# One hybrid decoder step: the projection taken by token groups, with the gates and the prompt chunks written between its weight slabs

## The chip, the cores and the metric

The kernel runs on one core of a Trainium2 chip. The metric is the time of one execution on the device in microseconds (us); the median of three runs is compared. The profile is one execution recorded instruction by instruction. TensorE is PE there (PEld its weight loads), VectorE is DVE, ScalarE is ACT, GpSimd is POOL, SyncE is SP.

## What is computed

One decoder layer for 2048 prompt tokens and 32 sample tokens (8 sequences of 4), 2080 in all, D = 1024:

```python
mq, mk, mv, mo, mi, mf, sq, sk, sv = split_in_proj(x @ w_in)      # 2816 columns and 8 gate columns
# group A: mLSTM, 4 heads of 128, in chunks, with a recurrent state C, n, m
logf = log_sigmoid(softcap(mf + b_fg)); b = cumsum(logf); m_row = max(b + m, max(logD))
h = (exp(b + m - m_row) * q @ C + (q @ k.T * exp(logD - m_row)) @ v) / max(|den|, exp(-m_row))
# group B: attention over a window of 128, 8 heads of 64, sinks and a relative bias
p = softmax_with_sink(q @ k.T / 8 + bias); o = p @ v
x = layer_norm(ALPHA * x + concat(rmsnorm(h) * g * sigmoid(mo), o) @ w_out)
x = layer_norm(ALPHA * x + (silu(x @ w_gate) * (x @ w_up)) @ w_ffn_out)
```

Outputs are x for all tokens and the states and window caches. All data is float32. The large products are made of three passes over a high and a low part of each operand: `hi*xh + hi*xl + lo*xh`, where `whi` is the weight rounded by ACT and `wlo` the rest, subtracted by POOL.

## The kernel before

Five programs follow each other, each with its own block and a barrier behind it.

`project` (lines 122 to 330) holds all 2080 tokens of x, split into `xh` and `xl`, in SBUF. The weights come once, as 22 slabs of 128 columns (512 KB each, two buffers of `raw`, `whi` and `wlo`); each slab meets the five token groups of 416 tokens (TG). So there are 5 gate products and 110 slab products, each of 24 matmuls (8 blocks of k, three passes, lines 267 to 269). DVE copies each result (L329), and SP stores whole rows of `projT` in DRAM.

`gates` turns the eight gate rows into the decay terms of all 16 prompt chunks: a chain of short operations on DVE and ACT, four transposes on PE, and the relative bias table (L557, L559). It writes `xsT` to DRAM and loads the first two chunks.

`prompt` is a loop over 16 chunks of 128 tokens. SP loads a chunk with four DMAs: `inp` (1280 KB in pieces of 512 B), `kwin`, `svT`, and `xs_b`, two rows of each head spread over all partitions (512 KB). These go one chunk pair ahead. Steps of chunk c+1 are written into chunk c to fill waits: its window scores (L723), exponentials (L822) and key transposes (L746). The state of a chunk enters the next.

`sample` does the same for the 32 sample tokens and fetches the first weights of the layer. `layer` (out projection, FFN, norms) is 338 slab products of the same kind, with the same two-buffer chain of load, ACT rounding and POOL subtraction. SP issues every load and nearly every store of the kernel, in order.

Of the kernel before, what the change touches and what calls it, by code (L numbers as in the profile page):

```python
# [43 lines left out]
HJ = 384  # L63
assert NG * TG == NT and NTT * TOK == TG
# [35 lines left out]
def gate_inputs(m):  # L100

    t = {n: m.sb(n, s) for n, s in (
        ("gi", [H * NC, C]), ("gf", [H * NC, C]), ("gi_s", [H, NS]), ("gf_s", [H, NS]),
        ("small", [H * NC, 4]), ("small_s", [H, 4]), ("m0_sb", [H, DB]))}
    t["loaded"] = m.sem("g_loaded")
    return t


def load_gates(sp, io, t):

    def get(dst, src):
        sp.dma_start(dst, src).then_inc(t["loaded"], 16)

    for i, (n, bias) in enumerate((("gi", "b_ig"), ("gf", "b_fg"))):
        get(t[n][:], bass.AP(tensor=io["gateT"].tensor, offset=i * H * NT, ap=[[NT, H], [C, NC], [1, C]]))
        get(t[n + "_s"][:], io["gateT"][i * H:i * H + H, SEQ:NT])
        get(t["small"][:, i:i + 1], bass.AP(tensor=io[bias].tensor, offset=0, ap=[[1, H], [0, NC], [1, 1]]))
        get(t["small_s"][:, i:i + 1], io[bias])
    get(t["m0_sb"][:], io["m0"])


def project(nc, io, gate_in):

    with ExitStack() as ctx:
        m = Store(nc, ctx)
        XK, XR = KD // 2, 3  # L130
        xh = m.sb("xh", [P, KD, NT], F32R)
        xl = m.sb("xl", [P, KD, NT], F32R)
        xraw = m.sb("xraw", [P, XR, XK, TG])
        graw = m.sb("graw", [P, KD, P])
        raw = m.sb("raw", [P, 2, KD, P])
        whi = m.sb("whi", [P, 2, KD, P], F32R)
        wlo = m.sb("wlo", [P, 2, KD, P], F32R)
        ghi = m.sb("ghi", [P, KD, P], F32R)
        glo = m.sb("glo", [P, KD, P], F32R)
        out = m.sb("out", [P, 2, NT])  # L140
        grow = m.sb("grow", [8, 2, TG])
        acc = [m.ps(f"acc{i}", [P, 512]) for i in range(8)]
# [24 lines left out]

        @block.sync
        def _(sp):
            def load(i, s):  # L170
                sp.dma_start(raw[:, s], io["wA"][bass.ds(i * 2 + s, 1)].rearrange("a p k n -> (a p) k n")).then_inc(raw_in[s], 16)

            def load_x(h):
                sp.dma_start(xraw[:, h % XR], io["xT"][h // 2, :, h % 2 * XK:h % 2 * XK + XK]).then_inc(x_in[h % XR], 16)

            def store(i, s, tiles=None):

                sp.wait_ge(acc_free, tiles or (i * 2 + s + 2) * NG)
                sp.wait_ge(g_in, 16)
                sp.dma_start(io["projT"][bass.ds(i * 2 + s, 1)].rearrange("a p n -> (a p) n"),  # L180
                             out[:, s]).then_inc(out_free[s], 16)

            def store_gates(g):
                sp.wait_ge(acc_free, 3 * g + 1)
                sp.dma_start(io["gateT"][:, g * TG:g * TG + TG], grow[:, g % 2]).then_inc(g_stored[g % 2], 16)

            for dst, src in ((relb, io["rel_bias"]), (onehot, io["c_onehot"]), (outside, io["c_outside"])):
                sp.dma_start(dst, src).then_inc(table_in, 16)
            load_x(0)
            sp.wait_ge(g_zero, 1)  # L190
# [12 lines left out]
            for s in range(2):
                sp.wait_ge(lo_done[s], 1)
                load(1, s)
            for g in range(NG - 2, NG):
                store_gates(g)
            for s in range(2):
                store(0, s, FIRST)
            for s in range(2):  # L210
                sp.wait_ge(g_stored[s], (NG + 1 - s) // 2 * 16)
            load_gates(sp, io, gate_in)
            with sp.Fori(2, ITER) as i:
                for s in range(2):
                    sp.wait_ge(lo_done[s], i)
                    sp.wait_ge(g_in, 16)
                    load(i, s)
                for s in range(2):
                    store(i - 1, s)
            for s in range(2):  # L220
                store(ITER - 1, s)

        @block.scalar
        def _(act):
            def round_x(h):
                act.wait_ge(x_in[h % XR], h // XR * 16 + 16)
                nc.scalar.activation(half(xh, h), xraw[:, h % XR], ACT.Copy).then_inc(x_hi, 1)

            round_x(0)
            act.wait_ge(g_in, 16)  # L230
            nc.scalar.activation(ghi[:], graw[:], ACT.Copy).then_inc(g_hi, 1)
            round_x(1)
            for s in range(2):
                act.wait_ge(raw_in[s], 16)
                nc.scalar.activation(whi[:, s], raw[:, s], ACT.Copy).then_inc(hi_done[s], 1)
            for h in range(2, 2 * NG):
                round_x(h)
            for s in range(2):
                act.wait_ge(raw_in[s], 32)
                act.wait_ge(acc_full, FIRST - 1 + s)  # L240
                nc.scalar.activation(whi[:, s], raw[:, s], ACT.Copy).then_inc(hi_done[s], 1)
            with act.Fori(2, ITER) as i:
                for s in range(2):
                    act.wait_ge(raw_in[s], i * 16 + 16)
                    act.wait_ge(acc_full, (i * 2 + s) * NG)
                    act.wait_ge(g_in, 16)
                    nc.scalar.activation(whi[:, s], raw[:, s], ACT.Copy).then_inc(hi_done[s], 1)  # L247

        @block.gpsimd
        def _(pool):  # L250
            nc.gpsimd.memset(graw[:], 0.0).then_inc(g_zero, 1)
            pool.wait_ge(g_hi, 1)
            nc.gpsimd.tensor_tensor(glo[:], graw[:], ghi[:].bitcast(F32), ALU.subtract).then_inc(g_split, 1)
            with pool.Fori(0, ITER) as i:
                for s in range(2):
                    pool.wait_ge(hi_done[s], i + 1)
                    nc.gpsimd.tensor_tensor(wlo[:, s], raw[:, s], whi[:, s].bitcast(F32),  # L257
                                            ALU.subtract).then_inc(lo_done[s], 1)

        @block.tensor  # L260
        def _(pe):
            def product(bank, hi, lo, g, halves=False):
# [1605 lines left out]
```

## Time and profile before

| | us |
|---|---|
| runs | 2704.88, 2705.39, 2707.74 |
| median | 2705.39 |
| span of the profiled execution (first to last instruction) | 2705.0 |
| PE busy of it | 2549.0 (94%) |
| PEld, DVE, ACT, POOL busy | 2466.6, 1062.1, 798.0, 1082.2 |
| DMA | 314.91 MB, mean 116 GB/s |

No time of its own is recorded for the profiled execution besides its span; the span is 0.4 us under the median, so what lies around it is small. The stages by time: projection to 535.2 us, gates to about 569, prompt to about 850, sample to about 892, layer from 901.9 to the end. Busy time of PE is an average over these stages, and each has another limit.

### The profile page before, as it was taken

The numbers are of one execution on the slowest core, as the hardware profiler recorded it, in microseconds if no ns is written. First come the engines' busy times: TensorE is split into PE (matmuls) and PEld (weight loads), VectorE is DVE, ScalarE is ACT, GpSimd is POOL, SyncE is SP. The second block draws the span as 40 slices with busy tenths as digits, with TensorE's granted clock in tenths as the row PEclk, the third lists the DMA queues.
The fourth block names the chain that finished last, engine by engine and source line by source line (L and its number), as shares of the span: only waits on it lengthen the run. The fifth ranks groups of instructions, "written<-read, shape, count | busy, mean of one in ns | idle before, by whom it ended". The sixth has DMA issues, their size and how long they took to land.

```text
span 2705.0 us, 39819 instructions
## 1 busy us (share of the span) xinstructions
PE 2549.0 (94%) x14173; PEld 2466.6 (91%) x14173; DVE 1062.1 (39%) x1723; ACT 798.0 (30%) x1270; POOL 1082.2 (40%) x462
## 2 busy tenths in 40 slices
PE   8999999958888779999999999999999999999996
PEld 8999999847776779999999999999999999999996
DVE  4111111147776243333553325644157341563403
ACT  2000000047885124422332223322224222242221
POOL 1111111012223335555455554555545555455553
PEclk9999999979998779999999999999999999999998
DMA  4212111176675314433344332443324433343332
GB/s 160 96 63 76 65 72 69 48 174 151 151 151 147 113 58 141 139 115 115 108 153 142 114 124 95 148 149 120 119 96 134 167 118 116 102 127 116 119 118 68
DMA packets 164636, 314.91 MB, mean 116 GB/s; under 512 B 16124, under 2 KB 111060, under 8 KB 161092
## 3 DMA queue, kind: packets, MB, share of 16 engines
q1 hardware_dynamic: 162224, 305.34, 36.3%
q10 hardware_dynamic: 2340, 8.52, 1.1%
q8 instruction: 57, 0.93, 0.1%
q14 instruction: 15, 0.12, 0.0%
HBM read 270.80 MB, written 44.17 MB: 116 GB/s over the span
## 4 chain that ended last, share of the span: by engine, by line
issue 39%; POOL 14%; PE 11%; DVE 1%; POOLq 1%; DMA 0%; ACT 0%; DVEq 0%
POOL l_wlo L1390 14%; PE l_acc L1512 4%; PE l_acc L1514 4%; PE l_acc L1513 4%; POOLq L1387 1%; DVE nrm L1641 0%; DVE stats L1632 0%; DMA out_y<-nrm 0%; POOLq L1389 0%; PE turned L1532 0%; DVE nrm L1739 0%; DVE nxt L1654 0%; DVE nxt L1650 0%; POOL al L1397 0%; DVE mv L1635 0%
## 5 line engine op out<-in xcount | busy, mean ns | idle before, releaser
L1390 POOL TENSOR_TENSOR l_wlo<-l_raw,l_whi 128x1024 fp32r<-128x1024 f32 (+1 forms) x338 | 906.4, 2682 | 848.9 <-ACT l_whi L1419 848.9
L1512 PE MATMUL l_acc<-ah,l_whi 128*128 128x416 f32 x2080 | 733.3, 353 | 23.6 <-DVEq L1613 9.9
L1514 PE MATMUL l_acc<-ah,l_wlo 128*128 128x416 f32 x2080 | 735.6, 354 | 0.0
L1513 PE MATMUL l_acc<-al,l_whi 128*128 128x416 f32 x2080 | 728.4, 350 | 0.0
L1419 ACT ACTIVATE l_whi<-l_raw 128x1024 fp32r<-128x1024 f32 (+1 forms) x338 | 384.9, 1139 | 1134.0 <-PE l_acc L1514 1100.8
L1512 PEld LDWEIGHTS l_acc<-ah,l_whi 128*128 128x128 f32 x2080 | 392.0, 188 | 29.0 <-POOL l_wlo L1390 10.3
L1513 PEld LDWEIGHTS l_acc<-al,l_whi 128*128 128x128 f32 x2080 | 392.4, 189 | 6.3
L1514 PEld LDWEIGHTS l_acc<-ah,l_wlo 128*128 128x128 f32 x2080 | 391.6, 188 | 2.7
L1512 PE MATMUL l_acc<-hh,l_whi 128*128 128x416 f32 x880 | 311.4, 354 | 7.5 <-POOL l_wlo L1390 2.9
L1514 PE MATMUL l_acc<-hh,l_wlo 128*128 128x416 f32 x880 | 309.9, 352 | 0.0
L267 PE MATMUL acc<-xh,whi 128*128 128x416 f32 x880 | 309.3, 351 | 0.0
L268 PE MATMUL acc<-xl,whi 128*128 128x416 f32 x880 | 308.2, 350 | 0.0
L269 PE MATMUL acc<-xh,wlo 128*128 128x416 f32 x880 | 308.1, 350 | 0.0
L1513 PE MATMUL l_acc<-hl,l_whi 128*128 128x416 f32 x880 | 307.4, 349 | 0.0
L1673 DVE TENSOR_TENSOR hbuf<-silu,l_acc 128x416 f32<-128x416 f32 x110 | 64.6, 587 | 501.2 <-PE l_acc L1514 501.2
L1678 DVE TENSOR_TENSOR hl<-hbuf,hh 128x416 f32 (+1 forms) x110 | 251.9, 2290 | 12.1
L257 POOL TENSOR_TENSOR wlo<-raw,whi 128x1024 fp32r<-128x1024 f32 x22 | 56.0, 2547 | 425.1 <-ACT whi L247 364.3
L329 DVE COPY out<-acc 128x416 f32<-128x416 f32 x100 | 59.2, 592 | 393.6 <-PE acc L269 389.5
L1512 PEld LDWEIGHTS l_acc<-hh,l_whi 128*128 128x128 f32 x880 | 165.2, 188 | 12.5 <-POOL l_wlo L1390 7.3
L1513 PEld LDWEIGHTS l_acc<-hl,l_whi 128*128 128x128 f32 x880 | 165.4, 188 | 2.3
L269 PEld LDWEIGHTS acc<-xh,wlo 128*128 128x128 f32 x880 | 165.1, 188 | 2.1
L268 PEld LDWEIGHTS acc<-xl,whi 128*128 128x128 f32 x880 | 165.3, 188 | 1.4
(295 smaller groups left out, 2413.0 us busy)
## 6 DMA issues: line engine op xcount, KB each, us to landing
l_raw<-in_wB SPq DMA_DIRECT2D x260, 512.0 KB, 3.4
l_raw<-in_w SPq DMA_DIRECT2D x80, 704.0 KB, 4.1
projT<-out SPq DMA_DIRECT2D x22, 1040.0 KB, 4.0
inp<-projT SPq DMA_DIRECT2D x16, 1280.0 KB, 6.7
raw<-in_wA SPq DMA_DIRECT2D x22, 512.0 KB, 5.4
xraw<-in_xT SPq DMA_DIRECT2D x10, 832.0 KB, 4.6
mixr<-mixT SPq DMA_DIRECT2D x5, 1664.0 KB, 8.9
nxt<-in_xT SPq DMA_DIRECT2D x5, 1664.0 KB, 7.8
```

Of the source, the lines that this page charges most:

```text
L257: nc.gpsimd.tensor_tensor(wlo[:, s], raw[:, s], whi[:, s].bitcast(F32), ALU.subtract).then_inc(lo_done[s], 1)
L267: pe.matmul(acc[bank][:, 0:TG], hi[:, k], xh[:, k, xs], start=(k == 0), stop=False)
L268: pe.matmul(acc[bank][:, 0:TG], hi[:, k], xl[:, k, xs], start=False, stop=False)
L269: last = pe.matmul(acc[bank][:, 0:TG], lo[:, k], xh[:, k, xs], start=False, stop=(k == KD - 1))
L329: nc.vector.tensor_copy(out[:, s, g * TG:(g + 1) * TG], acc[(n + NG) % 2][:, 0:TG]).then_inc(acc_free, 1)
L1390: nc.gpsimd.tensor_tensor(wlo[:, s, 0:k], raw[:, s, 0:k], whi[:, s, 0:k].bitcast(F32), ALU.subtract).then_inc(S["lo_done"], 1)
L1419: nc.scalar.activation(whi[:, s, 0:k], raw[:, s, 0:k], ACT.Copy).then_inc(S["hi_done"], 1)
L1512: pe.matmul(acc[:, bank, 0:TG], whi[:, s, c], hx[:, a], start=(a == 0), stop=False)
L1513: pe.matmul(acc[:, bank, 0:TG], whi[:, s, c], lx[:, a], start=False, stop=False)
L1514: last = pe.matmul(acc[:, bank, 0:TG], wlo[:, s, c], hx[:, a], start=False, stop=(a == total - 1))
L1673: nc.vector.tensor_tensor(hbuf[:], silu[:, s], acc[:, 2 * s + 1, 0:TG], ALU.mult).then_inc(S["evac"], 2)
L1678: nc.vector.tensor_tensor(hl[:, at], hbuf[:].unsqueeze(1), hh[:, at].bitcast(F32), ALU.subtract).then_inc(S["h_split"], 1)
```

## The change

`project`, `gates` and `prompt` become one program, `mixers`. The outer loop is the token group: 5 groups of 416 tokens, and for each the 22 weight slabs are loaded, rounded and split anew, so 110 slabs pass where 22 did. Only two groups of x are in SBUF; x is loaded and split in eight visits (`VISITS`). Of the gate weights only the eight real columns of each block are rounded and subtracted, the rest is set to zero. `raw` keeps two buffers, `whi`, `wlo` and `out` have three. A store is one slab of one group (208 KB).

Everything is written out, no loop is left. A slot n holds slab n (0 to 109) on every engine; five gate products stand before slabs 0, 3, 6, 9 and 12, for the groups 0, 4, 3, 2, 1. The gates' steps stand in slots 15 to 21. Each chunk is cut into six pieces (TURN, MIX, WIN, TURN2, VALUES, OUT), and a table says behind which slab each stands: chunks 0 to 8 take seven slots, chunks 9 to 15 five. Chunks are not interleaved with each other any more, except that OUT of one shares a slot with TURN of the next. Chunks 13, 14 and 15 have bases 110, 115 and 120: there are no slabs left there. `LOADS_AT` says in which slot SP loads a chunk; a chunk whose tokens end in group g is loaded after the last slab of g is stored.

In a slot, SP issues the slab four ahead, the store, then chunk loads; ACT rounds the slab three ahead, then does its pieces; POOL splits the slab three ahead, then its pieces; PE does the product, then its pieces. The Exp of `snk` stands before the Sqrt of `root`. PSUM tiles are fewer (`kd`, `fb`, `ce`, `w01`, two `acc`). The loads for `sample` go out in slot 90. `sample` and `layer` are as they were, at fixed SBUF addresses.

```diff
-def project(nc, io, gate_in):
...
-            with pe.Fori(1, ITER) as i:
-                for s in range(2):
-                    pe.wait_ge(lo_done[s], i + 1)
-                    for g in range(NG):
...
-                        product((n + NG) % 2, whi[:, s], wlo[:, s], g)
...
+VISITS = ((0, 0), (4, 1), (3, 1), (2, 1), (1, 1), (2, 0), (3, 1), (4, 0))
+SEVEN, FIVE = (0, 2, 3, 5, 6, 7), (0, 1, 2, 3, 4, 5)
+BASES = (24, 31, 38, 46, 53, 60, 68, 75, 82, 90, 95, 100, 105, 110, 115, 120)
+PIECES = tuple(tuple(b + o for o in (SEVEN if c < 9 else FIVE)) for c, b in enumerate(BASES))
+LOADS_AT = (21, 22, 28, 43, 44, 50, 65, 66, 72, 87, 88, 93, 98, 109, 110, 113)
+PREP_AT = tuple(b if c in (0, 3, 6, 9, 13) else b - 1 for c, b in enumerate(BASES))
...
+def mixers(nc, io, keep, outs, taken, at):
...
+            def load(n):
+                sp.dma_start(raw[:, n % 2], io["wA"][n % NPROJ]).then_inc(raw_in[n % 2], 16)
...
+            def load_chunk(c):
...
+                if c in (0, 3, 6, 9, 13):
+                    last = slab_tile((0, 3, 6, 9, 13).index(c) * NPROJ + NPROJ - 1)
+                    for k in range(last - 2, last + 1):
+                        landed(k)
+                sp.dma_start(inp[:, s], io["projT"][0:20, :, tok].rearrange("t p n -> p t n")).then_inc(loaded[s], 16)
...
+            for n in range(END):
+                if n < NSLAB:
...
+                    if n + 4 < NSLAB:
+                        sp.wait_ge(lo_done, n + 3)
+                        load(n + 4)
+                    store(n)
...
+            def round_slab(n):
+                act.wait_ge(raw_in[n % 2], n // 2 * 16 + 16)
+                if n >= 3:
+                    act.wait_ge(acc_full, slab_tile(n - 3) + 1)
+                nc.scalar.activation(whi[:, n % 3], raw[:, n % 2], ACT.Copy).then_inc(hi_done, 1)
...
+            for n in range(END):
+                if n + 3 < NSLAB:
+                    round_slab(n + 3)
...
+                for c in at_piece(n, OUT):
+                    out_turned(c)
+                for c in at_piece(n, TURN):
+                    turned(c)
...
+                for c in at_piece(n + 1, TURN):
+                    scale_queries(c)
```

SP at the first of the places where two chunk loads stand in neighbouring slots (43 and 44; the same at 21 and 22, 65 and 66, 87 and 88). `raw<-in_wA` is a weight slab, the four rows from `inp` to `xs_b` are one chunk. Before, from the end of one turn of the prompt loop:

```order
L348 DMA inp<-projT 128x20x128
L350 ISA
L350 DMA kwin<-projT 128x256
L352 ISA
L352 DMA svT<-projT 128x128
L357 DMA xs_b<-xsT 128x8x128
L652 ISA
L652 DMA mixT<-mixed 128x8x128
```

and now:

```order
L310 DMA inp<-projT 128x20x128
L312 DMA kwin<-projT 128x256
L317 DMA svT<-projT 128x128
L318 DMA xs_b<-xsT 128x8x128
L280 DMA raw<-in_wA 128x1024
L299 DMA projT<-out 128x416
L310 DMA inp<-projT 128x20x128
L312 DMA kwin<-projT 128x256
L317 DMA svT<-projT 128x128
L318 DMA xs_b<-xsT 128x8x128
L280 DMA raw<-in_wA 128x1024
L299 DMA projT<-out 128x416
```

A weight slab now stands behind a whole chunk in SP's queue, and another behind two.

ACT from the end of chunk 2 to the exponentials of chunk 3 (slots 42 to 46; the whi rows are the roundings of slabs 45 to 49). `whi<-raw` is a slab's rounding, `sq` the scaled queries that PE's TURN waits for, `pw` the window's exponentials, `mixed` the OUT copy. Before, in the loop:

```order
L858 ACTIVATE hn,ssq<-m 128x128 x4
L828 ACTIVATE ptw<-w2b 128x512
L863 ACT_TABLE_LOAD
L863 ACTIVATE root<-root 128x4
L865 ACT_TABLE_LOAD
L865 ACTIVATE snk<-snk 128x8
L866 ISA
L868 ACTIVATE mixed<-w2b 128x512
L641 ISA
L822 ACTIVATE pw,psums<-sw,nmx 128x256 x2
```

and now:

```order
L630 ACTIVATE whi<-raw 128x1024 x2
L651 ACTIVATE ptw<-w 128x512 x2
L630 ACTIVATE whi<-raw 128x1024 x2
L696 ACTIVATE mixed<-ce 128x512
L657 ACTIVATE sq_133<-inp 128x512
L630 ACTIVATE whi<-raw 128x1024
L663 ACTIVATE vaug<-ce 128x4x128
L641 ACT_TABLE_LOAD
L641 ACTIVATE pw,psums<-sw,nmx 128x256 x2
L669 ACTIVATE decay<-expo,ucol 128x128 x4
```

Each piece of a chunk on ACT now stands behind the rounding of the slab three ahead: `sq_133` behind that of slab 48, `vaug` and `pw` behind that of 49.

PE where one chunk passes into the next (chunk 12 into 13). `w<-kwin` are window scores, `fb<-vs` or `w3b<-vs` the values, `hn` and `ow` the two transposes of OUT, `inp` the transposes of keys and queries. Before:

```order
L723 MATMUL w<-kwin,sq 128x256 x4
L739 MATMUL w3b<-vs,ptw 128x64 x8
L746 MATMUL m0b<-ident,inp 128x128 x4
L798 MATMUL m3b<-ident,hn 128x128 x4
L802 MATMUL w2b<-ident,ow 128x128 x4
L754 MATMUL m<-ident,inp 128x128 x4
L757 MATMUL m<-inp 128x128 x4
```

and now, behind the last product:

```order
L470 MATMUL acc<-xh_64,wlo 128x416
L502 MATMUL fb<-vs,ptw 128x64 x8
L557 MATMUL kd<-ident,hn 128x128 x4
L563 MATMUL ce<-ident,ow 128x128 x4
L483 MATMUL w<-kwin,sq_133 128x256 x4
L516 MATMUL kd<-ident,inp 128x128 x4
L519 MATMUL fb<-ident,svT 128x128
L521 MATMUL ce<-ident,inp 128x128 x4
L525 MATMUL ce<-inp 128x128 x4
```

The next chunk's window scores and key transposes (`kd<-ident,inp`) stood ahead of OUT and now stand behind it.

## Rows read from the trace of the kernel before

**Rows 1.** Windows by stage: us, busy per engine (instructions), clock, DMA share, GB/s.

```profile
12.40:535.20 522.80, 522.68 (x2760) 517.01 (x2760) 86.14 (x124) 34.95 (x29) 55.92 (x22) 1.00 0.20 75
535.20:569.70 34.50, 7.12 (x17) 3.27 (x17) 9.67 (x42) 10.15 (x24) 3.26 (x10) 0.65 0.64 172
...
600.00:800.00 200.00, 171.87 (x1358) 144.88 (x1357) 149.51 (x518) 160.71 (x480) 54.65 (x48) 1.00 0.70 155
...
902.00:906.00 4.00, 4.00 (x12) 3.82 (x13) 0.00 (x0) 0.00 (x0) 0.00 (x0) 0.50 0.34 99
...
950.00:960.00 10.00, 5.72 (x25) 4.53 (x26) 9.10 (x17) 1.51 (x4) 1.94 (x1) 0.50 0.00 0
```

**Rows 2.** The first splits, in order of time: start, length, wait.

```profile
8.27 1.89 DVE L296 TENSOR_TENSOR xl<-xraw,xh 128x1664 fp32r<-128x1664 f32 x1 [2.32 <-ACT xh L227]
9.26 3.11 POOL L253 TENSOR_TENSOR glo<-graw,ghi 128x1024 fp32r<-128x1024 f32 x1 [7.57 <-ACT ghi L231]
```

**Rows 3.** Two operations of the gates' chain.

```profile
548.45 0.55 DVE L528 TENSOR_TENSOR b_s<-b_s,gf_s 4x8 f32<-4x8 f32 x3
...
551.23 0.18 DVE L537 TENSOR_TENSOR u_s<-gi_s,b_s 4x32 f32<-4x32 f32 x1
```

**Rows 4.** SP in order of time: a chunk load, a held issue, the last store.

```profile
557.10 9.95 SPq L350 DMA_DIRECT2D kwin<-projT  x1
...
627.11 0.38 SPq L348 DMA_DIRECT2D inp<-projT  x1
...
630.84 0.38 SPq L357 DMA_DIRECT2D xs_b<-xsT  x1
...
850.11 0.38 SPq L652 DMA_DIRECT2D mixT<-mixed  x1
```

**Rows 5.** DMA issues of gates and prompt: count, size, us to landing.

```profile
inp<-projT SPq DMA_DIRECT2D x16, 1280.0 KB, 6.7
xs_b<-xsT SPq DMA_DIRECT2D x16, 512.0 KB, 9.3
...
projT<-out SPq DMA_DIRECT2D x1, 1040.0 KB, 4.2
```

**Rows 6.** The layer around one large load: SP's issues, then ACT's wait.

```profile
1402.34 0.39 SPq L1347 DMA_DIRECT2D mixr<-mixT  x1
...
1406.02 0.34 SPq L1333 DMA_DIRECT2D l_raw<-in_wB  x1
...
1413.13 1.06 ACT L1419 ACTIVATE l_whi<-l_raw 128x1024 fp32r<-128x1024 f32 x1 [5.28 <-DMA l_raw<-in_wB]
```

**Rows 7.** Groups of projection and prompt: count, busy, mean ns, idle.

```profile
L329 DVE COPY out<-acc 128x416 f32<-128x416 f32 x100 | 59.2, 592 | 393.6 <-PE acc L269 389.5 <-DMA projT<-out 4.1
L257 POOL TENSOR_TENSOR wlo<-raw,whi 128x1024 fp32r<-128x1024 f32 x22 | 56.0, 2547 | 425.1 <-ACT whi L247 364.3 <-ACT whi L241 60.8
...
L822 ACT ACTIVATE pw<-sw,nmx 128x256 f32<-128x256 f32 x96 | 47.7, 499 | 14.4 <-DVE nmx L896 14.1
...
L863 ACT ACT_TABLE_LOAD x12 | 15.4, 1283 | 0.2
...
L695 POOL TENSOR_TENSOR expo<-xs_b,causal 128x512 f32<-128x512 f32 x12 | 15.3, 1274 | 2.6 <-DMA xs_b<-xsT 2.6
L839 ACT ACTIVATE decay<-expo,ucol 128x128 f32<-128x128 f32 x48 | 15.2, 389 | 0.0
```

**Rows 8.** PE: the last chunk's window scores, the sample's first.

```profile
827.40 1.14 PE L723 MATMUL w<-kwin,sq 64*128 64x256 f32 x8
...
852.84 0.37 PE L1120 MATMUL s_sc<-ident,s_inp 128*32 128x128 f32 x1 [3.50 <-PEq L591]
```

**Rows 9.** Neighbours in time on POOL and DVE in the first chunk.

```profile
588.92 1.04 POOL L702 TENSOR_TENSOR gate<-gate,gml 128x512 f32<-128x512 f32 x1
...
589.04 0.94 DVE L896 TENSOR_SCALAR nmx<-mx 128x2 f32<-128x2 f32 x1
...
833.32 0.17 DVE L896 TENSOR_SCALAR nmx<-mx 128x2 f32<-128x2 f32 x1
```

More of the change, by code:

```diff
@@ new lines, in mixers @@
+        own = t.sb("own", [R, C])
+        gx, gxs = t.sb("xs", [R, 2, C]), t.sb("xss", [H, 2, NS])
+        ones_r = t.sb("ones_r", [R, C])
+        m_last = t.sb("m_last", [H, DB])
+        m_end = t.sb("m_end", [1, H])
+        ends = t.sb("ends", [1, 2, H, NC])
+        after = t.sb("after", [1, H, NC])
+        before = t.sb("before", [1, H, NC])
+        inherited = t.sb("inherited", [R, 1])
+        anti = t.sb("anti", [P, P])
+        hank = t.sb("hank", [P, 8, 2 * W])
+        srow = t.sb("srow", [32, 132])
@@ L715, in _, with product @@
         @block.tensor
         def _(pe):
-            def window_scores(c, s, r):
-                wait(pe, "nmx_ready", c, r)
-                for g in range(2):
-                    gp = slice(64 * g, 64 * g + 64)
+            def product(k, hi, lo, v, split):
+                bank, x = acc[k % 2], VISITS[v][1]
+                if k >= 2:
+                    pe.wait_ge(acc_free, k - 1)
+                for a in range(KD):
+                    if split and a % XK == 0:
+                        pe.wait_ge(x_split, 2 * v + a // XK + 1)
+                    pe.matmul(bank[:, 0:TG], hi[:, a], xh[x][:, a], start=(a == 0), stop=False)
+                    pe.matmul(bank[:, 0:TG], hi[:, a], xl[x][:, a], start=False, stop=False)
+                    last = pe.matmul(bank[:, 0:TG], lo[:, a], xh[x][:, a], start=False, stop=(a == KD - 1))
+                last.then_inc(acc_full, 1)
@@ L722, in window_scores, with slab @@
+            def slab(n):
+                gr = n // NPROJ
+                pe.wait_ge(lo_done, n + 1)
+                product(slab_tile(n), whi[:, n % 3], wlo[:, n % 3], (0, 4, 5, 6, 7)[gr], n % NPROJ == 0)
+            def window_scores(c, r):
+                s = c % 2
+                for gr in range(2):
+                    gp = slice(64 * gr, 64 * gr + 64)
                     for a in range(2):
-                        last = pe.matmul(w01[:, g, a * 256:a * 256 + 256], sq8[gp, r + a], kwin[gp, s],
+                        last = pe.matmul(w01[:, gr, a * 256:a * 256 + 256], sq8[gp, r + a], kwin[gp, s],
@@ L774, in chunk @@
                 wait(pe, "kw_ready", c)
-                wait(pe, "pt_copied", c, 2)
-                for h in range(H):
-                    last = pe.matmul((m3, m0)[h // 2][:, (h % 2) * 129:(h % 2) * 129 + 129], kw[:, h], vaug[:, h],
-                                     start=True, stop=True)
-                last.then_inc(S["state_up"], 1)
-                wait(pe, "sv_ready", c)
-                window_values(c, s, 0)
-                turn_window(c, 2, w2)
-                window_values(c, s, 1)
@@ new lines, in mixed, with window, values @@
+                for h in range(H):
+                    last = pe.matmul(update[h], kw[:, h], vaug[:, h], start=True, stop=True)
+                last.then_inc(S["state_up"], 1)
+            def window(c):
+                wait(pe, "pt_copied", c, 2)
+                window_scores(c, 2)
+                wait(pe, "st_ready", c)
+                window_values(c, 0)
+                window_values(c, 1).then_inc(S["first_values"], 1)
+            def values(c):
+                window_values(c, 2)
+                window_values(c, 3).then_inc(S["swa_out"], 1)
@@ L803, in chunk @@
                 last.then_inc(S["o_turned"], 1)
-            pe.wait_ge(zeroed, 4)
-            pe.wait_ge(loaded[0], 64)
-            turn_keys(0, 0)
-            wait(pe, "sq_ready", 0)
-            window_scores(0, 0, 0)
-            with pe.Fori(0, NC // 2 - 1) as i:
-                for s in range(2):
-                    chunk(i, s, True)
-            for s in range(2):
-                chunk(NC // 2 - 1, s, s == 0)
+            pe.wait_ge(ext_table, 48)
+            pe.matmul(fb[0:8, 0:HJ], relb[:], onehot[:], start=True, stop=True).then_inc(ext_full, 1)
```

1232 lines of the change are left out of this document (602 added, 630 removed).

## The prediction, made before the changed kernel ran

> **What bounds the kernel now.** First the windows by stage [rows 1]. From 12.4 to 535.2 us PE is busy 522.68 of 522.80 us at granted clock 1.00, so the projection is PE's own work: 115 products, 4.546 us each. The DMA share is 0.20 there. The gates, to 569.7, are a chain of small operations: PE works 7.12 of 34.5 us at clock 0.65. The prompt is a loop of about 16.6 us a chunk (12 table loads, one a chunk, in 200 us [rows 7]); those 200 us have 171.87 us of PE, 144.88 of weight loads, 160.71 of ACT, and the DMA share is 0.70. So 28 us of 200 are waits of PE, and the chain of 34.5 us is nearly all wait. That is what placing this work between products can fill. Sample starts at 852.84 us [rows 8] and needs the last chunk's output; everything behind it, 1852.2 us to the end of the span of 2705.0, is untouched. So the whole question is when sample starts, against 852.8.
>
> **The start.** Before, PE's first product waited for `glo`, whose subtraction on POOL took 3.11 us from 9.26 [rows 2], to 12.4. Now only the eight real gate columns of each block are subtracted, so x's own split, ending at 8.27 + 1.89 = 10.16, is last: PE starts at about 10.3, 2.1 us earlier.
>
> **PE's work.** The 115 products stay, 522.8 us. A chunk's work costs between 12.1 us (weight loads, 144.88/12) and 14.3 (PE busy, 171.87/12). Busy includes matmuls that stand in the pipe while the next waits for its weights; in a piece that runs in one go behind a product, starts follow the weight loads. I take 12.1; the upper end would add 13 x 2.2 = 29 us. Behind slabs stand chunks 0 to 12; chunk 0 has no state and half a window (about 2.5 us less): 13 x 12.1 - 2.5 = 154.8. The gates' PE work is 7.12 us at clock 0.65, so 4.6 at full clock; I take 4.5. Sum: 10.3 + 522.8 + 154.8 + 4.5 = 692.4 us at the end of slab 109, with no wait at all. Before, chunk 12 is done only three chunks ahead of 850, near 800; so some 108 us are to be had at this point.
>
> **The other engines.** In a slot of 4.55 + 1.73 = 6.3 us ACT has a rounding (1.06 us [rows 6]) and a seventh of 13.4 us (160.71/12), POOL a split (2.547 us [rows 7]) and a seventh of 4.6, DVE a copy (0.592) and a seventh of 12.5. All stay under 60% on average. The sums don't bound; order can.
>
> **Loads.** One slab of 512 KB for each slot, besides the chunks: DMA goes from a share of 0.20 to about 0.65. That by itself fits. But a chunk load is issued from 627.11 to 630.84 [rows 4], 3.7 us, and its last part lands 9.3 us after issue [rows 5]: 13.0 us, of which about 10.5 are transfer (estimate: 16.6 us a chunk at share 0.70, less the stores). SP issues the load of slab n+4 behind it. Rows of the layer show what a load behind a large one does: `mixr` went out at 1402.34, `l_raw` at 1406.02, and ACT stood 5.28 us for `l_raw`, until 1413.13 [rows 6]: 7.1 us after issue. And with two chunk loads close together one issue, `kwin`, held SP 9.95 us [rows 4]. In the order of ACT, the scaled queries of chunk 3 stand behind the rounding of slab 48, its exponentials behind that of slab 49, and PE's TURN and MIX wait for these.
>
> **One pair of chunk loads, step by step** (slots 43 and 44, clock zero at the end of slot 43). The first load waits until the store of slab 43 has landed, about 3 us (1040 KB took 4.2 [rows 5]). It is issued to 6.7 and has landed at 16. Slab 48 stands behind it: landed 18, rounded 19, queries 19.6. PE wants them at TURN, behind product 46, at 2 x 6.3 + 4.55 = 17: it waits about 3. Chunk 4's load is next in line, 10.5 us of transfer; slab 49 lands at 29.5, is rounded at 30.6. Behind that come `vaug`, a table load (1.28 [rows 7]), eight `pw` of 0.5 and four `decay` of 0.39: 38. MIX stands behind product 48, at 29.7 + 3: it waits 5.5. So 9 us (rounded up) a pair, and there are four pairs. Slots 43/44 and 65/66: 18. Slots 21/22: the slots behind them have no pieces and last 4.55 instead of 6.3, so four slots give 7 us less cover, and the gates' chain of 34.5 us stands in seven slots of 4.55 (31.9): 3 late, in part the same wait; together 17. Slots 87/88: chunks of five slots, MIX one slot earlier, against longer slots: 13. The single loads in 93 and 98: 2 each, 4. Together 52 us. Behind long waits PE's clock falls: after sample it worked 4.00 of 4.00 us at 0.50 [rows 1], a loss of 2 us; four times that, 8. So 692.4 + 60 = 752.4. Of all terms this 60 is the least sure; 10 is its lower end (only the gates' chain and a little), 70 the upper.
>
> **The end.** Chunk 13 is loaded when the last slab is stored: copy and issue of `out` about 1.0 (the copy is 0.592 [rows 7]), landing 2.5 for 208 KB, load 13.0: 16.5 us with nothing beside them. To 768.9. Chunks 13, 14, 15 then have no product to cover their waits. Before's last chunk, from its window scores at 827.40 to the store at 850.11 [rows 8, 4], took 22.7 us without a next chunk beside it. In the new order the next chunk's window scores and key transposes stand behind OUT, so all three cost that: 68.1. PE is busy about half of it, and at 5.72 busy of 10 the clock was 0.50 [rows 1], so their 9 us of matmuls on the chain take 4.5 more each: 13.5. To 850.5. From the store to sample's first matmul 2.7: **853.2**, 0.4 later than before.
>
> So the span is 2705.4, and the median, 0.4 above the span before, 2705.8: I say **2706 us**. The gain between the slabs goes into waits of ACT's rounding, an open load and three uncovered chunks.
>
> **Rivals.**
> *A, the forecast*: slab loads stand in line behind chunk loads. For it: [rows 6] and the held issue. Its own range is 2690 to 2722 (waits of 45 to 70, tail of 20 to 25 a chunk).
> *B, the transfers share*: slabs overtake or share with the chunks, so the wait is 10 instead of 60, and sample starts at 803: **2656**. For it: the DMA queues are idle a third of the time, and a wait of 52 us was worked out from few rows, with a slack of three slots that needs only a few us more to hide all. Against it: in [rows 6] the later load landed after the earlier one.
> The Trainium skill ("DMA: Bandwidth & Descriptors", section "Queues, rings and completion order") says that each DMA engine takes descriptors in the order of its ring, though a later one may finish first, and speaks so against this change. The row of 5.28 us agrees; by strict order the waits are the 52 us, without it B.
> *C, slower*: POOL's split runs in every slot, 2.55 us long, and a small DVE operation beside a POOL operation stretches: `nmx` took 0.94 us beside `gate` of 1.04, against 0.17 else [rows 9]. Beside a split it may be held up to 2.4 us, and `nmx` gates the exponentials, those the transposes of TURN2 and VALUES. In 13 chunks once: 31 us more than A, **2737**. It decides only if `pw` is already later than PE: from about 3.8 us after the end of the slab. Against it: seven slots per chunk leave a slot between most pieces. The bound of 14.3 us a chunk for PE's work ends at the same time.
> The gates' small operations (0.55 and 0.18 us [rows 3]) are open to the same, but are counted as a chain already. That the pieces would not stand between slabs at all is excluded by the orders: the rounding and the pieces alternate.
>
> **How the numbers follow.** A 0.45, B 0.33, C 0.22. A measurement of this kernel tells about 0.2% (5.4 us) from no change. Of A, 0.12 falls below 2700, 0.15 within and 0.18 above 2711; B is all faster, C slower but for 0.02. So faster 0.45, same 0.17, slower 0.38. The range of 8 in 10 holds A, and most of B and of C: 2650 to 2738; A alone is 2690 to 2722.
>
> **What the changed profile would show.** Sample's first matmul near 853. PE's first product near 10.3. Before slab 109's end (at 752) PE waits of some 5 us at TURN and MIX of the chunks behind a pair, ended by ACT, with ACT's rounding waiting for DMA `raw`: if these are missing, B. `nmx` of 2 us and more beside `wlo`, and waits ended by it: C. Products that take more than 4.55 at clock 1.00 would break the PE term. Behind slab 109 a hole of some 16 us ended by DMA, then three chunks of 27 us at a clock of about 0.5; if they take 20, I am 20 us too slow. I am wrong in kind if the three-slab lookahead absorbs the chunk loads, or if waits stand where I have none (x's reload, `out`'s stores).

## The result: 63 us slower

The changed kernel takes 2769.7 us (median of 4 runs, 2767.8 to 2771.3) against 2706.2 before, now also the median of 4: a ratio of 1.0233, 95% interval 1.0218 to 1.0247. The forecast was 2706, the range 2650 to 2738. The span of its profiled execution is 2766.0 us, 61.0 more than before.

The first lines of the page, busy time of each engine, then the clock and DMA of the 40 slices:

```profile
PE 2579.0 (93%) x14173; PEld 2503.8 (91%) x14173; DVE 1112.3 (40%) x1729; ACT 897.1 (32%) x1364; POOL 1295.9 (47%) x551
...
PEclk9989999998986679999999999999999999999998
DMA  6546554638543423433244333443334433343332
```

A slice is 69 us. The clock row dips in slices 3, 10 and 12 and is lowest in 13 to 15, where the uncovered chunks, sample and the start of the layer stand. PE in order of time (start, length, and in brackets the wait and what ended it): the first product, the end of chunk 12 and the wait behind it, and sample's first matmul.

```profile
10.91 0.71 PE L468 MATMUL acc<-xh,ghi 128*128 128x416 f32 x1 [6.13 <-POOL glo L421]
...
810.13 0.66 PE L563 MATMUL ce<-ident,ow 128*128 128x128 f32 x4 [0.34 <-DVE ow L853]
827.16 2.08 PE L483 MATMUL w<-kwin,sq 64*128 64x256 f32 x8 [16.37 <-DMA xs_b<-xsT]
...
914.49 0.58 PE L1116 MATMUL s_sc<-ident,s_inp 128*32 128x128 f32 x2 [3.50 <-PEq L145]
```

Sample starts at 914.49 where it started at 852.84 [rows 8]: 61.65 us later, the whole difference. From there on the two kernels take the same time. Slab 109 ends at 807.4 and the work of chunk 12 at 810.8, not at 752.4 as I had it; behind that the way to sample is 3 us longer than forecast. The windows of the merged program: all of it to slab 109, what is behind it, one turn of seven slots in which PE never waits, two stretches at low clock, and one uncovered chunk (columns as in [rows 1]):

```profile
10.90:807.40 796.50, 729.33 (x4222) 697.76 (x4223) 312.16 (x727) 317.68 (x665) 333.71 (x173) 0.95 0.56 163
807.40:914.50 107.10, 68.37 (x366) 58.58 (x365) 34.09 (x133) 41.74 (x122) 13.79 (x13) 0.66 0.40 84
265.03:310.00 44.97, 44.97 (x283) 43.46 (x282) 18.72 (x50) 20.73 (x47) 21.14 (x11) 1.00 0.38 127
228.20:235.10 6.90, 4.47 (x20) 3.76 (x21) 2.20 (x6) 3.36 (x5) 5.01 (x4) 0.51 0.44 138
330.60:337.50 6.90, 6.30 (x27) 5.55 (x28) 2.27 (x11) 0.51 (x1) 1.92 (x1) 0.51 0.78 157
842.00:869.00 27.00, 20.73 (x109) 17.55 (x108) 10.53 (x42) 13.13 (x37) 3.87 (x4) 0.69 0.43 95
```

The third is the chunk at its best: 44.97 us for seven slots, less 7 x 4.546 for the products, leaves 13.15 us a chunk. The waits of PE ahead of slab 109 add up to 67.2 us in 19 places from 12 us on, the longest at TURN of chunk 0 (7.8), at TURN and MIX of chunk 9 (6.1, 6.4 and 2.0). Between 140 and 807 us there are 13 stretches at clock 0.50, 78.5 us in all; 20.9 of them are waits anyway, and half of the rest, 28.8 us, is what PE's work took longer there. I call this the lost clock.

How one wait comes about: TURN of chunk 1, behind slab 31. SP in order of time:

```profile
209.38 0.33 SPq L280 DMA_DIRECT2D raw<-in_wA  x1
...
210.39 0.37 SPq L310 DMA_DIRECT2D inp<-projT  x1
210.80 4.96 SPq L312 DMA_DIRECT2D kwin<-projT  x1
215.81 1.62 SPq L317 DMA_DIRECT2D svT<-projT  x1
217.47 0.44 SPq L318 DMA_DIRECT2D xs_b<-xsT  x1
217.96 0.58 SPq L280 DMA_DIRECT2D raw<-in_wA  x1
```

then ACT, and PE:

```profile
228.95 1.06 ACT L630 ACTIVATE whi<-raw 128x1024 fp32r<-128x1024 f32 x1 [12.45 <-DMA raw<-in_wA]
229.91 0.61 ACT L657 ACTIVATE sq<-inp 128x512 f32<-128x512 f32 x1
...
230.63 1.66 PE L483 MATMUL w<-kwin,sq 64*128 64x256 f32 x6 [5.69 <-issue]
```

The chunk load holds SP from 210.39 to 217.9; the slab load goes out at 217.96 and arrives 11.0 us later; ACT stands 12.45 us for it, and only then scales the queries that have nothing to do with that slab. PE, done with slab 31's product, waits 5.69 us for the queries. Then the clock is at 0.50 from 228.2 to 235.1.

### The profile page after: what moved, and what is told of

The parts are those of the page before. It is cut to its first block, busy times and chain, and to the rows that moved or that the text cites. A ratio compares the mean times of both kernels' runs of the same rounds, so it can differ in the third digit from the quotient of the medians.

```text
span 2766.0 us, 39383 instructions
## 1 busy us (share of the span) xinstructions
PE 2579.0 (93%) x14173; PEld 2503.8 (91%) x14173; DVE 1112.3 (40%) x1729; ACT 897.1 (32%) x1364; POOL 1295.9 (47%) x551
## 4 chain that ended last, share of the span: by engine, by line
issue 38%; POOL 14%; PE 11%; DVE 1%; POOLq 1%; DMA 0%; ACT 0%; DVEq 0%
POOL l_wlo L1386 14%; PE l_acc L1508 4%; PE l_acc L1510 3%; PE l_acc L1509 3%; POOLq L1383 1%; DVE nrm L1637 0%; DVE stats L1628 0%; DMA out_y<-nrm 0%; POOLq L1385 0%; PE turned L1528 0%; DVE nrm L1735 0%; DVE nxt L1650 0%; DVE nxt L1646 0%; POOL al L1393 0%; DVE mv L1631 0%
## 5 line engine op out<-in xcount | busy, mean ns | idle before, releaser
L399 POOL TENSOR_TENSOR wlo<-raw,whi 128x1024 fp32r<-128x1024 f32 x110 | 264.8, 2408 | 441.4 <-ACT whi L630 441.4
L468 PE MATMUL acc<-xh,whi 128*128 128x416 f32 x880 | 317.8, 361 | 0.0
L1674 DVE TENSOR_TENSOR hl<-hbuf,hh 128x416 f32 (+1 forms) x110 | 251.8, 2289 | 12.1
L630 ACT ACTIVATE whi<-raw 128x1024 fp32r<-128x1024 f32 x110 | 116.2, 1057 | 399.7 <-PE acc L470 214.4
L776 DVE COPY out<-acc 128x416 f32<-128x416 f32 (+1 forms) x115 | 67.8, 589 | 265.3 <-PE acc L470 264.9
L468 PEld LDWEIGHTS acc<-xh,whi 128*128 128x128 f32 x880 | 167.7, 191 | 1.4
```

Of the source, the lines that this page charges most:

```text
L399: nc.gpsimd.tensor_tensor(wlo[:, n % 3], raw[:, n % 2], whi[:, n % 3].bitcast(F32), ALU.subtract).then_inc(lo_done, 1)
L468: pe.matmul(bank[:, 0:TG], hi[:, a], xh[x][:, a], start=(a == 0), stop=False)
L630: nc.scalar.activation(whi[:, n % 3], raw[:, n % 2], ACT.Copy).then_inc(hi_done, 1)
L776: nc.vector.tensor_copy(out[0:rows, k % 3], acc[k % 2][0:rows, 0:TG]).then_inc(acc_free, 1)
L1674: nc.vector.tensor_tensor(hl[:, at], hbuf[:].unsqueeze(1), hh[:, at].bitcast(F32), ALU.subtract).then_inc(S["h_split"], 1)
```

## Experiments

Theory: the chunk loads make slab loads late, ACT stands for these, and chunk pieces stand behind ACT. Rivals: small operations of DVE and POOL beside the splits; or a DMA with no room for both. All ratios below are to the kernel before, run beside each of them on the same chip (medians 2707 to 2708). The changed kernel itself ran only in the first set, beside 2706, so differences to it are good to some 2 us at best.

**Chunk loads cut short.**

```diff
-  sp.dma_start(inp[:, s], io["projT"][0:20, :, tok]...)
+  rows = 20 if c < 2 or c > 12 else 1
+  sp.dma_start(inp[:, s, 0:rows], io["projT"][0:rows, :, tok]...)
```

`xs_b` likewise, one row of 8.

> Leaves out most of the loads of chunks 2 to 12: only one of 20 rows of inp and one of 8 rows of xs_b are loaded, so these chunks compute with old data; all else, orders and waits included, is as in the changed kernel. In the changed kernel PE waits 67.2 us before the end of slab 109 and works 28.8 us less than it would at full clock. Theory 1 (the loads make the waits, by standing before slab loads in SP's queue): the waits from chunk 1 on go, 49 us, and with them about 20 us of lost clock; left are those at chunk 0 (about 18 us). Time 2769.7 - 69 = 2700. Rival (waits come from the small operations of DVE and POOL beside the splits): waits stay, 2765 or more.

2697.1 us, ratio 0.9964 (0.9950 to 0.9978), near the 2700 of the theory. Waits ahead of slab 109: 21 us. Of the low stretches there, only the two at chunk 0 are left, with 4.4 us lost. The rival of DVE and POOL falls: their work is all still there.

**Four buffers for slabs.**

```diff
-  raw = m.sb("raw", [P, 2, KD, P])
+  raw = m.sb("raw", [P, 4, KD, P])
...
-  if n + 4 < NSLAB:
+  if n + 6 < NSLAB:
       sp.wait_ge(lo_done, n + 3)
-      load(n + 4)
+      load(n + 6)
```

> Four buffers of raw in place of two, slab n+6 loaded in slot n in place of n+4; nothing else. Every slab load goes out two slots (12 us) earlier than now against the same chunk load. Theory 1 (slab loads late because they stand behind a chunk load of 10 to 13 us): all waits under 8 us go, those at chunks 0 and 9 leave about 15 us together: waits 67 to 15, lost clock 29 to 8, time 2769.7 - 73 = 2697. Rival (the DMA has not the room for both, so earlier issue only shifts): waits stay at 50 or more, time 2755 or more.

2693.0 us, ratio 0.9948 (0.9931 to 0.9964), with every load back. The waits are 18 us and the lost clock 3.5: the wait at chunk 0 stays,

```profile
169.09 2.08 PE L487 MATMUL w<-kwin,sq 64*128 64x256 f32 x8 [8.15 <-ACT sq L661]
...
595.24 1.42 PE L487 MATMUL w<-kwin,sq 64*128 64x256 f32 x8 [3.13 <-DMA xs_b<-xsT]
```

and what is left at chunks 3, 6 and 9 (1.4, 1.3, 3.1) is the chunk's own load. So nearly the whole price of the loads, 77 us with the clock, was the slabs' lead and not the bytes: 8 KB a partition more of buffers take it away.

**Three buffers.**

```diff
+  raw = m.sb("raw", [P, 3, KD, P])
+  if n + 5 < NSLAB: ... load(n + 5)
```

> Three buffers of raw, slab n+5 in slot n. One slot more of lookahead is 6.3 us in the seven-slot part, so by theory 1 each wait is shorter by that: of 5.7, 3.9+3.0, 3.8, 3.7+3.4, 2.4 hardly any is left, of 14.4 at chunk 9 about 7, of 6.8 at MIX of 0 about 2: waits 67 to 25, lost clock 29 to 12: 2711. If only the number of buffers in flight mattered and not the slots of lead, it would be as with four: 2693.

2709.8 us, ratio 1.0003 (0.9994 to 1.0013); waits 29 us. That is the 2711 worked out with one slot of lead more. Each slot counts: 2769.7, 2709.8, 2693.0 for two, three and four buffers. The first slot is worth 60 us, the second 17.

**Other places for the same loads.**

```diff
-LOADS_AT = (21, 22, 28, 43, 44, 50, 65, 66, 72, 87, 88, 93, 98, 109, 110, 113)
+LOADS_AT = (21, 26, 33, 43, 48, 55, 65, 70, 77, 87, 91, 96, 101, 109, 110, 113)
```

> LOADS_AT alone: the loads of chunks 1, 2, 4, 5, 7, 8 go out two slots behind the TURN of the chunk before (26, 33, 48, 55, 70, 77), those of 10 to 12 in 91, 96, 101, so that none stands beside another or just ahead of a TURN. Same transfers, same number, other places. Theory 1: the waits at TURN of 1, 4, 7 (12 us) and at MIX of 0, 3, 6 (13 us) go, and half of those of 9 to 11 (11 us); with the clock about 15: 2769.7 - 51 = 2719. Rival (bandwidth or the other engines): within 10 us of 2770.

2718.3 us, ratio 1.0040 (1.0025 to 1.0054). The table alone gives back 51 us of the 63. Waits 35 us: the TURN waits of 3, 6 and 9 stay (3.7, 3.7, 5.9), since their slots are bound to the end of a group; new ones of 2.1 and 4.8 come at VALUES of two chunks, for `ptw` of ACT.

**Slab loads issued by ACT** in place of SP.

```diff
-  load(n + 4)
+  act.wait_ge(lo_done, n + 3)
+  act.dma_start(raw[:, (n + 4) % 2], io["wA"][(n + 4) % NPROJ])...
```

> The changed kernel with two buffers, but ACT issues the slab loads itself, behind the rounding in its slot, in place of SP: same loads, same slot, another queue. Theory 1 in the sharper form (a slab load is late because it stands behind the chunk load in SP's queue and behind SP's held issues, not because the DMA has no room): it lands in 7 us or less while a chunk load runs, waits 67 to about 20, time near 2700. Rival (shared bandwidth): it lands 9 to 11 us after issue as now, waits 50 or more, 2755 or more.

2707.8 us, ratio 1.0001 (0.9992 to 1.0011); waits 31 us. This is as good as a third buffer, and nearer to the theory than to the rival. But its sharper form holds for some loads only. At chunk 2's load, ACT in order of time, then SP:

```profile
203.80 0.33 ACTq L708 DMA_DIRECT2D raw<-in_wA  x1
214.39 1.06 ACT L627 ACTIVATE whi<-raw 128x1024 fp32r<-128x1024 f32 x1 [8.57 <-DMA raw<-in_wA]
```

```profile
197.88 0.37 SPq L310 DMA_DIRECT2D inp<-projT  x1
198.29 3.54 SPq L312 DMA_DIRECT2D kwin<-projT  x1
...
202.37 1.24 SPq L318 DMA_DIRECT2D xs_b<-xsT  x1
```

At the median a slab load of the changed kernel takes 3.9 us (page, DMA issues):

```profile
raw<-in_wA SPq DMA_DIRECT2D x110, 512.0 KB, 3.9
```

This one goes out at 203.80, 5.9 us behind `inp` and 1.4 behind `xs_b` on the other queue, and arrives 10.6 us later; in the changed kernel it went out 7.6 us behind `inp` and 0.5 behind `xs_b` and took 11.0. At chunk 8's load it is otherwise. ACT and SP again:

```profile
502.11 0.33 ACTq L708 DMA_DIRECT2D raw<-in_wA  x1
```

```profile
498.06 0.37 SPq L310 DMA_DIRECT2D inp<-projT  x1
...
502.83 0.45 SPq L318 DMA_DIRECT2D xs_b<-xsT  x1
```

Here ACT's load goes out 4.0 us behind `inp` but ahead of `xs_b`, and lands in 5.7 us. The same slab's load (77) in the changed kernel went out 4.2 us behind `inp`, just behind `xs_b`, and took 12.5. The other places agree. In this run eight slab loads went out up to 4.9 us behind `inp` and ahead of `xs_b`: they took 5.6 to 7.2 us. Six went out 0.9 to 3.7 us behind `xs_b`: 10.5 to 11.3 us; six further behind it took 5.6 to 9.5. In the changed kernel all 22 that went out with `xs_b` in flight landed after it, and took 9.0 to 14.3. So another queue does not let a slab past `xs_b`. What it saves is the place in the order: a slab load that SP's held `kwin` no longer keeps back goes out ahead of `xs_b`. I ran no kernel that only moves `xs_b` behind the slab loads on SP's own queue, so how much that would give is open.

**Rounding behind the queries**, on ACT in the slot before each TURN.

```diff
-  round_slab(n + 3)
   ...
   scale_queries(c)
+  round_slab(n + 3)
```

> The changed kernel, but in the slot before each TURN ACT scales the queries first and rounds the slab three ahead behind them; no other edit, two buffers, same loads. This takes ACT's place in the chain alone away: the slab is as late as before, but the queries don't stand behind it. Expected: waits at TURN of 1, 4 and 7 (11.9 us) go whole, those of 3, 6 and 9 (13.7) by half, as the chunk's own load lands 1 to 2 us before; MIX's waits stay (its exponentials still stand behind the next rounding). Time 2769.7 - 22 = 2748. Rival (PE would only wait for the late slab itself a slot later): above 2762.

2770.0 us, ratio 1.0233 (1.0209 to 1.0257): nothing. The queries do come earlier: TURN of chunks 3, 6 and 9 waits 0.9, 0.9 and 3.5 us, where it waited 3.9, 3.7 and 6.1. But the wait comes back behind it. TURN of chunk 1 starts on time, and PE waits 4.27 us further on in the same piece, and more at MIX of chunk 3:

```profile
231.98 1.42 PE L525 MATMUL ce<-inp 128*128 128x128 f32 x7 [4.27 <-ACT mixed L696]
...
345.23 1.09 PE L493 MATMUL w<-ident,pw 128*128 128x128 f32 x4 [5.95 <-ACT pw L641]
```

`mixed` and `pw` are ACT's too and stand behind the next rounding. MIX of chunk 3 waited 0.5 first, now 5.95. The expectation missed the second operation behind the same slab; here the earlier slab helps, and the order of ACT's pieces does not.

**PE kept busy in its waits.** Filling matmuls before TURN and MIX, into the free product bank:

```diff
+  def warm(n, count):
+      pe.wait_ge(acc_free, slab_tile(n + 1) - 1)
+      pe.wait_ge(hi_done, n + 2)
+      for _ in range(count):
+          pe.matmul(acc[...], whi[:, (n + 1) % 3, 0], xh[x][:, 0], start=True, stop=True)
```

> Before TURN of chunks 0, 1, 3, 4, 6, 7 and 9 and MIX of 0, 3, 6 and 9, PE does 12 to 40 matmuls of a next slab's weights into the product bank that is free (0.19 us each, overwritten by the next product), about as long as the wait there; nothing else. Theory (each wait costs its length and then a stretch at clock 0.50, 28.8 us in all): PE's waits are filled, the waits for the data stay in time, but the granted clock stays at 1.00 at these places: some 20 us less, 2750. Rival (the clock falls there for another reason, or the filling pushes PE behind the data): 2768 to 2780, with low clock at the same places.

2772.1 us, ratio 1.0234 (1.0215 to 1.0253): no gain. The low stretch at 228 is gone, but I had filled too much: the filling ahead of MIX of chunk 0 (L486) itself waits for a bank whose copy stands on DVE behind `prob` and `kw`, and these behind ACT's `decay`.

```profile
194.04 2.45 PE L486 MATMUL acc<-xh,whi 128*128 128x416 f32 x6 [10.44 <-DVE out L788]
```

This run decides nothing. Again with less:

> The changed kernel with filling matmuls again, now fewer than the wait holds and none at chunk 0 nor at MIX of 3 and 6: 25, 14, 15, 13, 8 and 27 before TURN of 1, 3, 4, 6, 7 and 9, 24 before MIX of 9. They can't push what follows. Theory (a wait costs its own length once more in clock): lost clock 28.8 to about 14 at these places, time 2769.7 - 13 = 2757. Rival (clock falls for another reason): 2769.

2765.9 us, ratio 1.0222 (1.0207 to 1.0236). Lost clock fell by 13 us, to 16.0, but the time by 3.8 and the ratio by 0.0011, less than the width of either interval: a gain in time is not shown. PE at MIX of chunk 3, in the changed kernel:

```profile
346.95 0.63 PE L493 MATMUL w<-ident,pw 128*128 128x128 f32 x4 [0.53 <-ACT pw L641]
350.06 0.63 PE L493 MATMUL w<-ident,pw 128*128 128x128 f32 x4 [2.48 <-ACT pw L641]
```

and here:

```profile
346.90 0.63 PE L503 MATMUL w<-ident,pw 128*128 128x128 f32 x4 [2.65 <-ACT pw L653]
349.96 1.09 PE L503 MATMUL w<-ident,pw 128*128 128x128 f32 x4 [2.43 <-ACT pw L653]
```

PE arrives 2.1 us earlier and goes on at the same moment, when the exponentials come. In the changed kernel about 18 of the 28.8 us of lost clock stood ahead of a wait that lasted until data landed. There the filling shortened the clock's loss and lengthened the wait. The profiles show it slab by slab. After chunk 0, where nothing was filled, PE is 3.0 us behind the changed kernel (TURN waited 10.3 and not 7.8). Behind the filling at TURN of chunk 1 it is 1.0 behind, and with that of chunk 4 it is 0.7 ahead. At the end of slab 109 it is 0.3 behind. So 13 us of clock gave 2.7 us of time there.

**Early loads for the first chunk of a group** (3, 6, 9, 13), on top of four buffers. `load_most` loads `inp` and `xs_b` behind the landing of row 19, and `load_chunk` then only `kwin` and `svT`:

```diff
+  if c in EARLY and LOADS_AT[c] - 1 == n:
+      load_most(c)
   if LOADS_AT[c] == n:
       load_chunk(c)
```

> Four buffers of raw, and for chunks 3, 6, 9 and 13, the first of a token group, inp and xs_b are loaded one slot earlier: their 20 rows are stored two slabs before the group's end, only kwin and svT need the last two. Against the four-buffer kernel alone (2693.0, waits of 16.2 us behind slab 109 and of 1.4, 1.3 and 3.1 at TURN of 3, 6, 9, each ended by xs_b). Theory 1: the load of 13 us has no need to start so late; the 16.2 become about 6 (copy, store, kwin), the others go with 3 us of lost clock: 2674. Rival (kwin or svT, or the store before them, is what lands last): 2688 or more.

2678.7 us, ratio 0.9892 (0.9876 to 0.9908). The wait behind slab 109 went from 16.2 to 9.2, not to 6. (Chunk 0's `inp` goes out behind row 19 too by this edit; the wait at its TURN fell from 8.15 to 3.8.) SP in order of time, and PE:

```profile
721.00 2.69 SPq L316 DMA_DIRECT2D xs_b<-xsT  x1
725.57 1.21 SPq L299 DMA_DIRECT2D projT<-out  x1
734.21 0.33 SPq L328 DMA_DIRECT2D kwin<-projT  x1
```

```profile
737.26 2.08 PE L505 MATMUL w<-kwin,sq 64*128 64x256 f32 x8 [9.22 <-DMA svT<-projT]
```

The last store goes out at 725.57 and has landed only by 734.2, when SP goes on: 8.6 us for 208 KB, with `xs_b` in flight. So:

```diff
+  if c in EARLY and LOADS_AT[c] - 4 == n:
+      load_xs(c)
```

> As the kernel with four buffers and early inp (2678.7, 9.2 us of wait behind slab 109), but xs_b of chunks 3, 6, 9 and 13 is issued three slots before inp. In that kernel the store of slab 109 stood behind inp and xs_b and landed 8.6 us after its issue. Theory: what is in flight ahead of the store makes it late, and with xs_b gone it lands in 3 to 5 us: wait 9.2 to about 4.5, 2674. Rival (inp alone holds it as long): 2678.

2670.3 us, ratio 0.9859 (0.9842 to 0.9875):

```profile
725.02 0.32 SPq L299 DMA_DIRECT2D projT<-out  x1
727.50 0.32 SPq L329 DMA_DIRECT2D kwin<-projT  x1
```

```profile
730.63 1.66 PE L508 MATMUL w<-kwin,sq 64*128 64x256 f32 x6 [3.15 <-DMA svT<-projT]
```

The store now takes 2.5 us, and the wait is 3.15; the time is below the 2674 expected.

**Filling in the uncovered chunks**, on top of that:

```diff
+  def fill(c, count):
+      if c >= 13:
+          pe.wait_ge(acc_free, GATES + NSLAB)
+          for _ in range(count):
+              pe.matmul(acc[0][:, 0:TG], whi[:, 0, 0], xh[...][:, 0], start=True, stop=True)
```

> As e9_xs, and in chunks 13, 14 and 15, which no product covers, PE fills its waits: 11 matmuls of 0.19 us before MIX's first transposes, 5 before its second, 4 at TURN2, 6 at VALUES, into a product bank that nobody reads any more. Prediction's step (4.5 us a chunk of lost clock, on the chain): three chunks shorter by 13 us in all, 2661 if e9_xs is 2674. Rival (PE's slower work lies beside waits for ACT and DVE, and only makes these waits shorter): within 3 us of e9_xs.

2654.3 us, ratio 0.9803 (0.9787 to 0.9819), 16.0 us less. One uncovered chunk, without and with the filling (windows):

```profile
766.00:793.00 27.00, 21.34 (x113) 18.17 (x113) 10.69 (x43) 13.04 (x39) 4.57 (x4) 0.68 0.07 20
```

```profile
773.00:795.00 22.00, 19.29 (x139) 16.38 (x137) 10.66 (x43) 13.56 (x40) 2.08 (x2) 1.00 0.09 25
```

The windows are cut to 27 and 22 us; from TURN to TURN chunk 14 takes 22.0 us (750.81 to 772.80) at clock 1.00 with 26 matmuls more, and 27.9 (758.99 to 786.85) at 0.68 without them. Here the lost clock is on the chain, as the prediction had it. And the same in the changed kernel, with nothing else:

> The changed kernel with nothing but the filling matmuls in the waits of chunks 13 to 15. With four buffers and early loads this gave 16 us (2670.3 to 2654.3). If it is the clock in the three uncovered chunks and stands by itself, it gives the same 16 here: 2754. If it needed the better loads ahead of it: 2765 or more.

2760.6 us, ratio 1.0188 (1.0168 to 1.0208): 9 us less by the medians, 12 by the ratios, between the two expectations. In its profile

```profile
817.41 0.66 PE L571 MATMUL ce<-ident,ow 128*128 128x128 f32 x4 [0.34 <-DVE ow L863]
904.57 0.58 PE L1126 MATMUL s_sc<-ident,s_inp 128*32 128x128 f32 x2 [3.50 <-PEq L145]
```

are 87.2 us from the end of chunk 12 to sample, against 104.4 in the changed kernel (810.13 to 914.49): 17 us, as with the better loads. But the part ahead, in which nothing was edited, came out 7.3 us longer (2.6 of it at TURN of chunk 0, which waits 10.4 us and not 7.8), and the part from sample on 3.6 longer. Why these differ between executions by that much is open, and so is how much of the 17 us the time would show without it.

## The prediction, point by point

| | forecast | profile after | more |
|---|---|---|---|
| PE's start | 10.3 | 10.91 | 0.6 |
| the 115 products, 4.546 each | 522.8 | 525.5: the first took 7.2 | 2.7 |
| chunks 0 to 12 on PE, without waits and lost clock | 154.8 | 173.0 | 18.2 |
| the gates on PE | 4.5 | 5.4 | 0.9 |
| waits to the end of slab 109 | 52 | 67.2 | 15.2 |
| lost clock there | 8 | 28.8 | 20.8 |
| chunk 12 done (forecast: with slab 109) | 752.4 | 810.8 | 58.4 |
| open load of chunk 13 | 16.5 | 16.4 | -0.1 |
| three uncovered chunks | 81.6 | 83.8 | 2.2 |
| from there to sample | 2.7 | 3.5 | 0.8 |
| sample | 853.2 | 914.5 | 61.3 |

From sample on nothing changed, as forecast. A run's time is 1.8 us over its span (2767.83 and 2766.0), not the 0.4 that I added.

**The mechanism was right, and its price was not.** What I called A is what happens: ACT's rounding waits for `raw`, the pieces behind it are late, and the terms of the sum stand in the profile one by one: chunk 0 and the gates ahead of it with 16.6 us for 17, the pairs at chunks 3 and 6 with 6.9 and 7.1 for 9, chunk 9 with 14.4 for 13. The step "the single loads in 93 and 98: 2 each" was mis-sized (4.6 and 3.9), and it put the single loads in 28, 50 and 72 at nothing, without a reason given. These stand just ahead of TURN of chunks 1, 4 and 7 and cost 5.7, 3.8 and 2.4. My sum counted loads close to each other; what counts is where the rounding of a slab whose load is late meets a piece. The three that were left out are 11.9 of the 15.2 us.

**The clock** was the largest error: "four times that, 8". I priced it for the long waits alone. Thirteen stretches came, behind waits of 1.9 us as well as behind 7.8. The price by subtraction is not additive, though: the filling at seven of these places took away 13 us of lost clock and gave 2.7 of time. So 20.8 in the table is what stands in this execution, and taken away by itself it would bring less.

**A chunk's work** of 12.1 was the busy time of the weight loads. The profile has 12.9 to 13.6 us a chunk, 13.15 in the turn without waits, so 13.7 us more for 13 chunks. Window scores, with 256 columns for each load, don't follow the weight loads: before's last chunk shows for the same eight matmuls 1.14 us on PE [rows 8] and

```profile
827.40 0.74 PEld L723 LDWEIGHTS w<-kwin,sq 64*128 64x128 f32 x8 [0.17 <-issue]
```

Twice 0.4 is 0.8 of the 1.05 that were missing. The bound of 14.3 was in the text; the value was taken too near the low end. And chunk 0 is not 2.5 us cheaper. It does the state's matmuls like every other,

```profile
192.12 0.64 PE L537 MATMUL ce<-state,qs 128*128 128x129 f32 x2
```

and its seven slots hold 13.0 us of work.

**Rival B** was not what happened, but the run with four buffers shows what its condition is worth: 22 us of waits and lost clock for its 10, and 2693 for its 2656, most of the rest being the chunks' work, priced too low there as well. **Rival C** had the right side and the wrong cause. `nmx` does stretch, the first of these beside POOL's `qs` and the second beside the split,

```profile
233.79 1.13 DVE L790 TENSOR_SCALAR nmx<-mx 128x2 f32<-128x2 f32 x1
235.76 1.52 DVE L790 TENSOR_SCALAR nmx<-mx 128x2 f32<-128x2 f32 x1
```

but with short chunk loads, or with four buffers, the same operations run beside the same splits and PE hardly waits from chunk 1 on.

**The rule of the Trainium skill** ("DMA: Bandwidth & Descriptors", "Queues, rings and completion order"), that each DMA engine takes descriptors in the order of its ring, pointed the right way: what is issued behind a chunk load is late. The run with ACT's queue shows that behind `xs_b` it is late on another issuer's queue too, 10.6 us for 11.0, so the order of one ring is not the cause by itself; issued ahead of `xs_b` there it took 5.7.

**The range** was too narrow because the three errors of size, waits, clock and a chunk's work, point the same way and the upper bound of only one of them stood in it: waits of 70 (with the clock) where 96 came, 12.1 where the bound was 14.3. Both bounds together, 692.4 + 29 + 70, would have given 2745, and still not the result.

## To carry on

When work is put between streamed weights, count for each engine what stands behind the wait for the next weight, and ask how many slots of lead the load has against the longest transfer ahead of it. Here one buffer more was worth 60 us and two 77. Another place for the same loads gave 51, and another issuer for the slabs 62. Price every wait of TensorE with the slower stretch behind it, but only where no wait for data follows. Where a stage is left uncovered, filling matmuls in its waits can be worth more than they take, here 16 us: with four buffers, early loads and filling the same design takes 2654.3 us, 0.9803 of the kernel before.

## What the runs showed of the hardware

- A load of 512 KB takes 3.9 us to land at the median of the changed kernel, but 11.0 us behind `inp` and `xs_b` of a chunk load on the same queue and 10.6 behind them on another engine's queue. Behind `inp` alone, on that other queue, it took 5.7.
- A store of 208 KB took 8.6 us to land with a 512 KB broadcast (`xs_b`) and a 1280 KB load in flight, and 2.5 us with the latter alone, which landed 1.8 us after the store's issue.
- One `kwin` issue held SP 4.96 us, and 0.32 us with nothing in flight.
- Each wait of PE of 2.5 to 8 us from the gates on had a stretch of 3.4 to 10.2 us at granted clock 0.50 (1.2 GHz) beside or behind it, and so had one of 1.9; that of 2.43 at TURN of chunk 7 had none.
- In the uncovered chunks (20.73 of 27 us busy) the clock was 0.69 on average; with their waits filled it was 1.00 (2.4 GHz).
- Eight matmuls of 256 columns each took 1.14 us on PE where their weight loads were busy 0.74.
